# One decoder step on one core: the stick-breaking attention steps in another order, and one cast moved from DVE to ACT

## The chip, the cores and the metric

The kernel runs on one core of a Trainium2 chip. The metric is the device time of one execution, in microseconds. Before the change it is 2921.88 us, the median of three runs (2920.06 to 2928.34). All times below are in microseconds unless marked ns.

## The reference

The reference is one inference step of a small decoder with two layers. Layer 0 mixes tokens with a gated matrix product over chunks of 128 tokens, layer 1 with stick-breaking attention over keys and values shared by the layers of its kind; each is followed by a SwiGLU feed-forward layer. There are 1024 prompt tokens and 32 sample tokens (8 sequences of 4), a width of 1024, 16 heads of 64 and a hidden width of 2816. Everything is float32. The part that the change touches is the attention:

```python
z = jnp.einsum('bthd,bshd->bhts', q, k) * (HEAD_DIM ** -0.5) + bias     # scores
causal = k_pos[None, :] < q_pos[:, None]
log_beta = jax.nn.log_sigmoid(z)
log_rest = jnp.where(causal, jax.nn.log_sigmoid(-z), 0.0)
after = lax.cumsum(log_rest, axis=3, reverse=True) - log_rest
a = jnp.where(causal, jnp.exp(log_beta + after), 0.0)
out = jnp.einsum('bhts,bshd->bthd', a, v)
```

The weight of a key is exp(z - softplus(z) - the sum of softplus over all later keys). So each query needs a sum over the later keys, which the kernel forms with triangular matrices of -1 on TensorE, from the latest block of keys to the earliest.

## The kernel before

**Precision.** Each float32 matrix product is made of three products of fp32r parts: high by high, high by low, low by high. Who makes a high part rounds it with a copy or an activation, and who makes the low part subtracts the high part from the original. So each tile costs two elementwise passes, and each weight slab three on POOL (`w_hi`, the scaled `w_raw`, `w_lo`; lines 632 to 639).

**Stages.** The feed-forward layer of layer 0 ends at about 1150 us, the first key, query and value slab follows, attention runs from about 1187 to 2020, and the output projection and the second feed-forward layer fill the rest.

**The attention stage.** The 16 heads are worked on in 8 pairs. A pair has 12 steps s = 0 to 11 (`STEPS`, line 109). A step takes one block of 128 keys against up to 512 queries of the upper half (steps 0 to 7) or lower half (8 to 11) of the prompt, for two heads at once. Blocks on the diagonal are narrower: the widths are 128, 256, 384, 512, then 512 four times, then 128, 256, 384, 512. A tile of both heads has so 256 to 1024 elements in a partition. Each pair step is written out by hand for each engine, in a function `pair` of each, and the engines meet only at semaphores. For step s the chain is:

- PE `scores(s)` into PSUM (line 871)
- ACT `biased(s)`: scale and bias, into `zb` (1232)
- DVE `capped(s)`: minimum with 40, into `sp` (1553)
- ACT `exp_part(s)`, `log_part(s)`: the softplus, in place (1249, 1255)
- DVE `softplus(s)`: maximum with `zb` (1559)
- DVE `softplus_split(s)`: the cast to the high part (1570) and the low part by subtraction (1572), into `sp_part`
- PE `take_later(s)`: the triangular product of both parts, added to the running sums in PSUM (889)
- DVE `logits(s)`: that PSUM tile plus `zb` (1578)
- PE `carry(s)`: completes the block's contribution to the running sums (901), needs `logits(s)` to have read them
- ACT `weights(s)`: two exponentials, one to the high part in `a_part`, one in place (1242, 1243)
- POOL `a_low(s)`: the low part of the weights (644)
- PE `values(s)`: weights by values (916)

`sp_part` and `a_part` have one buffer each: the next high part of softplus may be written only when `carry` of the step before has read the last one, and the next `weights` only when `values` of the step before is done.

**Other work among the steps.** While one pair is in attention, PE projects the keys, queries and values of the next one, in nine chunks ("c" items, line 963, 24 matrix products of 384 or 288 columns each), turns key pages of the cache ("p"), and turns the projected keys and values to rows for output ("k", "v"). The tables `X1` and `X2` place these items in the steps: `X1` before `take_later`, `X2` behind it. DVE evicts each chunk (`chunk_evicted`, 1592) and makes low parts (`k_low`, 1604); ACT copies turned items and makes high parts (`k_high`, 1270). All items use one PSUM bank, `aux[:, 0]`, so an item can't begin before DVE or ACT has emptied the one before. POOL prepares the weight slabs in thirds (`split_part`) between its `a_low`. The 32 sample tokens have their own small chain (`sample`, `sample_values`, the `S_` constants). The last pair projects nothing; it restores earlier outputs instead (`o_back`, lines 1093 and 649).

The order within one step of a pair, before the change:

- PE: scores(s), values(s-3), carry(s-2), X1 item, take_later(s-1), X2 item, sample part
- ACT: biased(s), weights(s-2), exp_part(s), k_high, other copies, log_part(s), X2 item's copy
- DVE: logits(s-2), softplus(s-1), k_low, capped(s), cast and subtraction of s-1, chunk_evicted(s)
- POOL: a_low(s-2), a third of a slab in some steps

Lines of the PE, ACT and DVE programs with their numbers:

Of the kernel before, what the change touches and what calls it, by code (L numbers as in the profile page):

```python
# [23 lines left out]
ALU = mybir.AluOpType  # L24
# [58 lines left out]
def freed_by():  # L83
# [10 lines left out]
    for q0, t0 in zip(Q_FFN, T_FFN):  # L94
# [35 lines left out]
S_CAP, S_LOG, S_SOFT, S_LATER, S_EXP, S_VALUES = 8, 8, 9, 9, 10, 11  # L130
# [22 lines left out]
def yoco_step(nc, x_prompt, x_sample, cache_k, cache_v, page_table, norm_mix_g, a_w_in, a_v_g, a_ws, a_bs, a_w_out,  # L153
# [4 lines left out]
    with ExitStack() as ctx:  # L158
# [364 lines left out]
        def _(pool):  # L523
# [94 lines left out]
            gp.affine_select(out=s_mask[:], in_=s_mask[:], pattern=[[-DL, DB], [0, 2], [0, DL]], compare_op=ALU.is_ge,  # L618
                             fill=MASKED, base=0, channel_multiplier=1).then_inc(s_mask_done, 1)
# [32 lines left out]
            def pair(i, at, last_slabs=False, more=True):  # L652
                p, c = 2 * i + at, at % 2
                q = Q_KQV + 3 * (at + 1)
                for s in range(NS + (0 if more else 2)):
# [7 lines left out]
                    if more and s in (8, 9, 10):  # L663
                        split_part(s - 8, i, q + 3, None if last_slabs else G_KV, scaled + 3 * p + 2, 9 * p + 6)
# [21 lines left out]
        def _(pe):  # L686
# [311 lines left out]
            def sample_values(p, c):  # L998
                pe.wait_ge(s_ad, p + 1)
                pe.wait_ge(vp_in, 16 * DB * PAGES * (p + 1))  # L1000
                mm(os_, v_row[0:RS, RT, :], s_a[0:RS, 2, :], start=True, stop=False, skip_group_check=True)
                for n in range(DB * PAGES):
# [4 lines left out]
                last.then_inc(s_pv, 1)  # L1007

            def pair(p, c, more=True):
                for s in range(NS + (0 if more else 3)):  # L1010
                    if s < NS:
                        scores(p, c, s)
                    for lag, work in ((3, values), (2, carry)):
                        at = lagging(p, c, s, lag)
                        if at is not None:
                            work(*at)
                    if s in X1 and (more or X1[s][0] == "p"):
                        x_turn(p, c, X1[s], more)
                    if s == S_VALUES:
                        sample_values(p, c)  # L1020
# [5 lines left out]
                    sample(p, c, s)  # L1026

# [34 lines left out]
        def _(act):  # L1062
# [258 lines left out]
            def pair(p, c, more=True):  # L1321
                act.wait_ge(bias_done, p + 1)
                for s in range(NS + (0 if more else 3)):
# [21 lines left out]
                    if s == V_SPLIT:  # L1345
                        v_high(p)
# [56 lines left out]
        def _(dve):  # L1403
# [157 lines left out]
            def softplus_split(p, c, s):  # L1561
# [3 lines left out]
                if s > 0 and s - 1 in CARRY:  # L1565
                    dve.wait_ge(carry_done, NCARRY * p + CARRY.index(s - 1) + 1)
                elif s > 0 or not isinstance(p, int) or p > 0:
# [164 lines left out]
```

## Time and profile before

| What | Value |
|---|---|
| Median of three runs | 2921.88 us |
| The profiled execution's own time | 2921.54 us |
| Its span, first to last instruction | 2919.5 us |
| Mean granted TensorE clock | 0.955 of full speed |
| PE busy | 2763.1 us, 95% |
| DVE, ACT, POOL busy | 1350.9, 755.1, 1205.0 us |
| DMA engines, share of the span | 15.9% in the largest queue |

The span is one execution on the core; the device time has 2.0 us around it. PE busy is the time in which a matrix product was in the array, at whatever clock was granted. Idle time of an engine costs something only if the engine at the end of the chain waits for it. The granted clock has two levels, 2.4 GHz (1.00) and 1.2 GHz (0.50); a mean between them says for what share of a stretch it stood at the lower.

### The profile page before, as it was taken

The page shows a single profiled execution, that of the slowest core. Times are in us where ns is not written, and L with a number is a line of the kernel's source. Part 1 is how long each engine was busy: PE and PEld are TensorE (multiplying, and loading weights), DVE is VectorE, ACT ScalarE, POOL GpSimd, SP SyncE. Part 2 cuts the span into 40 slices and gives each one's busy share as a digit, 9 for nine tenths or more (in the row PEclk, how much of TensorE's full clock was granted, in tenths as well). Part 3 has the DMA queues.
Part 4 walks back from the last instruction along what each step waited for, and adds up shares of the span by engine and source line. Part 5 has one row for each costly group of instructions (what it writes and reads, how often), then busy time and mean ns, then how long its engine had stood idle before and what let it go on. Part 6 is the DMA issues. An engine that isn't in the chain of part 4 may idle for free.

```text
span 2919.5 us, 41661 instructions
## 1 busy us (share of the span) xinstructions
PE 2763.1 (95%) x16657; PEld 2637.8 (90%) x16657; DVE 1350.9 (46%) x1237; ACT 755.1 (26%) x1080; POOL 1205.0 (41%) x542
## 2 busy tenths in 40 slices
PE   7999999999999999899999999967999999999997
PEld 6989999999999999788787878756999999999997
DVE  5244543333333337566766766663543333333335
ACT  5122210000000002456665655653110000000003
POOL 4542454334433343344444444443454333433340
PEclk9999999999999999899988989966999999999999
DMA  3111111111111112221221122121121111111111
GB/s 111 51 31 37 44 58 45 51 44 44 44 51 44 44 44 94 61 61 39 64 60 36 53 66 63 32 91 67 43 59 44 46 50 44 44 44 51 44 37 60
DMA packets 219619, 152.91 MB, mean 52 GB/s; under 512 B 9258, under 2 KB 207714, under 8 KB 219426
## 3 DMA queue, kind: packets, MB, share of 16 engines
q1 hardware_dynamic: 200930, 139.63, 15.9%
q10 hardware_dynamic: 18496, 10.49, 1.2%
q8 instruction: 147, 2.41, 0.4%
q14 instruction: 46, 0.38, 0.0%
HBM read 128.86 MB, written 21.22 MB: 51 GB/s over the span
## 4 chain that ended last, share of the span: by engine, by line
PE 83%; DVE 6%; issue 5%; POOL 3%; ACT 2%; DMA 0%; ACTq 0%; SPq 0%; POOLq 0%; DVEq 0%
PE ps L706 48%; PE ps L835 17%; PE aux L963 6%; PE ps L889 2%; PE ps L916 2%; DVE sp_part L1572 2%; PE ps L871 2%; PE ps L901 2%; POOL a_part L644 1%; DVE scratch L1423 1%; PE aux L935 1%; PE aux L1005 1%; DVE sp_part L1570 1%; DVE sp L1559 1%; POOL w_raw L634 1%
## 5 line engine op out<-in xcount | busy, mean ns | idle before, releaser
L564 POOL TENSOR_TENSOR w_hi<-w_raw,ones_col 128x1024 fp32r<-128x1024 f32 x146 | 281.1, 1925 | 997.6 <-PE ps L706 674.2
L571 POOL TENSOR_TENSOR w_lo<-w_raw,w_hi 128x1024 fp32r<-128x1024 f32 x167 | 467.6, 2800 | 13.1
L644 POOL TENSOR_TENSOR a_part<-zb,a_part 128x256 fp32r<-128x256 f32 (+2 forms) x96 | 200.9, 2093 | 466.3 <-ACT zb L1243 466.3
L706 PE MATMUL ps<-near_hi,w_hi 128*128 128x352 f32 x1632 | 356.9, 327 | 17.0 <-DVE near_lo L1410 13.1
L706 PE MATMUL ps<-near_lo,w_hi 128*128 128x352 f32 x1632 | 354.2, 325 | 0.0
L706 PE MATMUL ps<-near_hi,w_lo 128*128 128x352 f32 x1632 | 352.8, 324 | 0.0
L706 PEld LDWEIGHTS ps<-near_hi,w_hi 128*128 128x128 f32 x1632 | 278.8, 190 | 21.1 <-issue 11.5
L706 PE MATMUL ps<-in_hi,w_hi 128*128 128x352 f32 x1320 | 286.6, 325 | 4.8 <-issue 3.9
L1537 DVE TENSOR_TENSOR h<-h,ps 128x1056 f32<-128x1056 f32 x160 | 200.2, 1251 | 187.3 <-PE ps L835 187.3
L706 PE MATMUL ps<-in_lo,w_hi 128*128 128x352 f32 x1320 | 285.3, 324 | 0.0
L706 PE MATMUL ps<-in_hi,w_lo 128*128 128x352 f32 x1320 | 283.9, 323 | 0.0
L706 PEld LDWEIGHTS ps<-near_hi,w_lo 128*128 128x128 f32 x1632 | 281.0, 189 | 0.0
L706 PEld LDWEIGHTS ps<-near_lo,w_hi 128*128 128x128 f32 x1632 | 279.2, 189 | 0.0
L1433 DVE TENSOR_TENSOR up<-ps,r_row 128x1056 f32<-128x1056 f32 x44 | 55.3, 1258 | 442.1 <-PE ps L706 442.1
L1193 ACT ACTIVATE gate<-gate 128x1056 f32<-128x1056 f32 x44 | 47.9, 1089 | 807.5 <-DVE gate L1433 807.5
L706 PEld LDWEIGHTS ps<-in_hi,w_hi 128*128 128x128 f32 x1320 | 224.7, 189 | 7.2 <-issue 5.3
L835 PE MATMUL ps<-hid_hi,w_hi 128*128 128x352 f32 x1056 | 228.4, 324 | 0.3 <-DVE h L1490 0.3
L835 PE MATMUL ps<-hid_lo,w_hi 128*128 128x352 f32 x1056 | 227.7, 324 | 0.0
L835 PE MATMUL ps<-hid_hi,w_lo 128*128 128x352 f32 x1056 | 227.2, 323 | 0.0
L706 PEld LDWEIGHTS ps<-in_hi,w_lo 128*128 128x128 f32 x1320 | 226.0, 188 | 0.0
L706 PEld LDWEIGHTS ps<-in_lo,w_hi 128*128 128x128 f32 x1320 | 224.8, 188 | 0.0
L1433 DVE TENSOR_TENSOR gate<-ps,r_row 128x1056 f32<-128x1056 f32 x44 | 55.3, 1258 | 320.0 <-PE ps L706 320.0
(218 smaller groups left out, 4501.2 us busy)
## 6 DMA issues: line engine op xcount, KB each, us to landing
w_raw<-in_w_gate_dram SPq DMA_DIRECT2D x44, 512.0 KB, 3.8
w_raw<-in_w_up_dram SPq DMA_DIRECT2D x44, 512.0 KB, 3.8
w_raw<-in_w_down_dram SPq DMA_DIRECT2D x44, 512.0 KB, 3.6
w_raw<-in_a_w_in_dram SPq DMA_DIRECT2D x16, 512.0 KB, 3.9
k_page<-in_cache_k_dram SPq DMA_DIRECT2D x128, 64.0 KB, 1.9
v_page<-in_cache_v_dram SPq DMA_DIRECT2D x128, 64.0 KB, 1.9
h_kept<-h SPq DMA_DIRECT2D x8, 528.0 KB, 2.7
h<-h_kept SPq DMA_DIRECT2D x8, 528.0 KB, 7.3
```

Of the source, the lines that this page charges most:

```text
L564: gp.tensor_tensor(hi, raw, one, ALU.mult).then_inc(w_hi_done, 1)
L571: gp.tensor_tensor(lo, raw, as32(hi), ALU.subtract).then_inc(w_ready, 1)
L644: gp.tensor_tensor(a_part[:, 1, :, c0:TB], zb[:, s % 3, :, c0:TB], as32(a_part[:, 0, :, c0:TB]), ALU.subtract).then_inc(a_split, 1)
L706: last = mm(out[:, c, 0:CH], w[:, ks], x[:, k, c * CH:c * CH + CH], start=(k == 0 and n == 0), stop=(k == KT - 1 and n == 2))
L835: last = mm(out[:, c, 0:CH], w[:, ns], x[:, buf, f, c * CH:c * CH + CH], start=(f == 0 and m == 0), stop=(f == 1 and m == 2))
L871: last = mm(ps[:, e, c0:TB], kq[rows, c, kn, P * j:P * j + P], kq[rows, c, qn, TB * b + c0:TB * b + TB], start=(m == 0), stop=(m == 2 and ...
L889: last = mm(ps[:, 2 + e, c0:TB], neg_tri_r[:], sp_part[:, x, e, c0:TB], start=(first and x == 0), stop=(x == 1), skip_group_check=True)
L901: last = mm(ps[:, 2 + e, c0:TB], neg_rest_r[:], sp_part[:, x, e, c0:TB], start=False, stop=(x == 1), skip_group_check=True)
L916: last = mm(ps[:, 4 + e, c0:TB], v_part[:, j, 2 * e:2 * e + 2, :].rearrange("p n d -> p (n d)"), a_part[:, x, e, c0:TB], start=(first and ...
L963: last = mm(xb[:, 0:CW[chunk]], w[:, ks], x[:, k, cols], start=(k == 0 and m == 0), stop=(k == KT - 1 and m == 2), skip_group_check=True)
L1433: vec.tensor_tensor(chunks(dst), ps[:, 3 * par:3 * par + 3, 0:CH], chunks(r_row[:]), ALU.mult)\
L1537: vec.tensor_tensor(chunks(h[:, n, :]), chunks(h[:, n, :]), ps[:, 3 * (n % 2):3 * (n % 2) + 3, 0:CH], ALU.add).then_inc(tile_out, 1)
```

## The change

The same reordered attention steps, and the cast of softplus to its high part on ACT instead of DVE. The order within one step of a pair after it:

- PE: scores(s), X1 item, half of the sample values in step 11, take_later(s-1), X2 item, sample part, the other half of the sample values in step 10, values(s-2), carry(s-1)
- ACT: weights(s-2), the cast `softplus_high(s-1)`, biased(s), exp_part(s), k_high, other copies, log_part(s), X2 item's copy
- DVE: softplus(s-1), the subtraction of s-1, v_low, capped(s), out, the sample's two, k_low, chunk_evicted(s), logits(s-1), sample_out
- POOL: as before, but the third slab's thirds stand in steps 7, 8, 9 and no longer in 8, 9, 10; and the three instructions that make the sample mask stand ahead of the five slabs of the first keys, queries and values

In the diff the first `pair` is PE's, `softplus_high` and the loop behind it are ACT's, and the last two parts are DVE's `softplus_split` and `pair`. The items of the tables `X1` and `X2` move too: chunks 5 to 7 and page item 3 come a step earlier, step 6 has now a chunk and a page item, step 9 has no chunk.

```diff
-X1 = {0: ("c", 0), 1: ("p", 1), 2: ("c", 1), 3: ("c", 2), 4: ("c", 3), 5: ("c", 4), 6: ("p", 3), 7: ("c", 5),
-      8: ("c", 6), 9: ("c", 7), 10: ("c", 8)}
-X2 = {0: ("p", 0), 2: ("k", 0), 3: ("k", 1), 4: ("k", 2), 5: ("p", 2), 9: ("v", 0), 10: ("v", 1), 11: ("v", 2)}
+X1 = {0: ("c", 0), 1: ("p", 1), 2: ("c", 1), 3: ("c", 2), 4: ("c", 3), 5: ("c", 4), 6: ("c", 5), 7: ("c", 6),
+      8: ("c", 7), 10: ("c", 8)}
+X2 = {0: ("p", 0), 2: ("k", 0), 3: ("k", 1), 4: ("k", 2), 5: ("p", 2), 6: ("p", 3), 8: ("v", 0), 9: ("v", 1),
+      11: ("v", 2)}
...
-S_CAP, S_LOG, S_SOFT, S_LATER, S_EXP, S_VALUES = 8, 8, 9, 9, 10, 11
+S_CAP, S_LOG, S_SOFT, S_LATER, S_EXP, S_VALUES = 8, 8, 9, 9, 10, (10, 11)
...
             ffn_splits(0)
-            for n in range(2):
-                scaled += 1
-                split(Q_KQV + n, 0, 0, n, (G_KV, G_MIX1)[n], scaled, 4 if n == 0 else 2)
-            for n in range(2, 5):
-                scaled += 1
-                split(Q_KQV + n, 0, 0, n % 2, (G_KV, G_MIX1, G_KV)[n % 3], scaled, 4 if n == 2 else 2)
-
-            pool.wait_ge(tile_done, T_KQV)
-            pool.wait_ge(sq_added, 4 * KT)
+            pool.wait_ge(sq_added, 3 * KT)
             gp.memset(s_mask[:], 0.0).then_inc(s_mask_done, 1)
...
+            for n in range(2):
+                scaled += 1
+                split(Q_KQV + n, 0, 0, n, (G_KV, G_MIX1)[n], scaled, 4 if n == 0 else 2)
...
...
-                    if more and s in (8, 9, 10):
-                        split_part(s - 8, i, q + 3, None if last_slabs else G_KV, scaled + 3 * p + 2, 9 * p + 6)
+                    if more and s in (7, 8, 9):
+                        split_part(s - 7, i, q + 3, None if last_slabs else G_KV, scaled + 3 * p + 2, 9 * p + 6)
...
             def pair(p, c, more=True):
-                for s in range(NS + (0 if more else 3)):
+                for s in range(NS + (0 if more else 2)):
                     if s < NS:
                         scores(p, c, s)
-                    for lag, work in ((3, values), (2, carry)):
-                        at = lagging(p, c, s, lag)
-                        if at is not None:
-                            work(*at)
                     if s in X1 and (more or X1[s][0] == "p"):
                         x_turn(p, c, X1[s], more)
-                    if s == S_VALUES:
-                        sample_values(p, c)
+                    if s == S_VALUES[1]:
+                        sample_values(p, c, 1)
...
                     sample(p, c, s)
+                    if s == S_VALUES[0]:
+                        sample_values(p, c, 0)
+                    for lag, work in ((2, values), (1, carry)):
+                        at = lagging(p, c, s, lag)
+                        if at is not None:
+                            work(*at)
...
+            def softplus_high(p, c, s):
+                b, j, c0 = STEPS[s]
+                if s > 0 and s - 1 in CARRY:
+                    act.wait_ge(carry_done, NCARRY * p + CARRY.index(s - 1) + 1)
+                elif s > 0 or not isinstance(p, int) or p > 0:
+                    act.wait_ge(c_done, NS * p + s)
+                act.wait_ge(sp_done, NS * p + s + 1)
+                nc.scalar.copy(sp_part[:, 0, :, c0:TB], sp[:, s % 2, :, c0:TB]).then_inc(sp_hi_done, 1)
...
-                    for lag, work in ((0, biased), (2, weights), (0, exp_part)):
+                    for lag, work in ((2, weights), (1, softplus_high), (0, biased), (0, exp_part)):
                         at = lagging(p, c, s, lag) if lag or s < NS else None
                         if at is not None:
                             work(*at)
+                        if s == V_SPLIT and work == weights:
+                            v_high(p)
...
-                vec.tensor_copy(hi, z).then_inc(sp_hi_done, 1)
                 dve.wait_ge(sp_hi_done, NS * p + s + 1)
                 vec.tensor_tensor(lo, z, as32(hi), ALU.subtract).then_inc(sp_split, 1)
...
-                for s in range(NS + (0 if more else 2)):
-                    for lag, work in ((2, logits), (1, softplus)):
-                        at = lagging(p, c, s, lag)
-                        if at is not None:
-                            work(*at)
+                for s in range(NS + (0 if more else 1)):
+                    at = lagging(p, c, s, 1)
+                    if at is not None:
+                        softplus(*at)
+                        softplus_split(*at)
+                    if s == V_SPLIT:
+                        v_low(p)
+                    if s < NS:
+                        capped(p, c, s)
+                    if s == OUT0 and (not isinstance(p, int) or p > 0):
+                        out(p - 1, 0)
+                    if s == OUT1:
+                        out(p, 1)
...
                         k_low(p, c, CHUNK_STEP[s - 2])
-                    if s < NS:
-                        capped(p, c, s)
-                    at = lagging(p, c, s, 1)
-                    if at is not None:
-                        softplus_split(*at)
                     if more and s in CHUNK_STEP:
                         chunk_evicted(p, c, CHUNK_STEP[s])
...
+                    if at is not None:
+                        logits(*at)
-                    if s == S_VALUES:
+                    if s == S_VALUES[1]:
                         sample_out(p)
```

## Rows read from the trace of the kernel before

**Rows 1.** Windows: pair 0, pair 6, the last pair; columns named in the first line.

```profile
core 0: us, PE busy (x) PEld busy (x) DVE busy (x) ACT busy (x) POOL busy (x), PEclk, DMA share, GB/s
1187.00:1290.00 103.00, 97.60 (x563) 86.05 (x564) 62.23 (x88) 58.97 (x98) 38.72 (x18) 0.87 0.15 42
...
1804.00:1905.00 101.00, 90.57 (x537) 77.76 (x535) 67.82 (x90) 61.55 (x101) 41.96 (x19) 0.92 0.19 55
1905.00:2020.00 115.00, 76.98 (x297) 59.03 (x297) 70.56 (x67) 61.45 (x86) 48.95 (x21) 0.62 0.28 92
```

**Rows 2.** PE's waits, 1187 to 2020: total us, times, longest.

```profile
PE ps L889 <- DVE sp_part L1572: 72.2, 33, 7.5
```

**Rows 3.** PE in order of time: start, us; idle before and releaser in brackets.

```profile
1186.52 0.91 PE L871 MATMUL ps<-kq 64*128 64x128 f32 x6 [4.53 <-POOL s_mask L618]
...
1541.66 2.07 PE L889 MATMUL ps<-sp_part,neg_tri_r 128*128 128x512 f32 x4 [4.29 <-DVE sp_part L1572]
```

**Rows 4.** Chain of waits through step 5 of pair 3: start, us, piece.

```profile
1525.70 0.89 PE ps L871 x6
1526.59 0.90 PE ps L916 x4
1527.49 0.92 PE ps L901 x4
1528.42 4.18 PE aux L963 x24
1532.60 0.94 PE ps L889 x4
```

**Rows 5.** ACT in order of time, the same step.

```profile
1527.48 1.26 ACT L1232 ACTIVATE zb<-ps,pair_bias 128x512 f32<-128x512 f32 x2 [1.22 <-PE ps L871]
1528.63 1.06 ACT L1242 ACTIVATE a_part<-zb 128x1024 fp32r<-128x1024 f32 x1
1529.58 1.05 ACT L1243 ACTIVATE zb<-zb 128x1024 f32<-128x1024 f32 x1
1530.53 1.05 ACT L1249 ACTIVATE sp<-sp 128x1024 f32<-128x1024 f32 x1
...
1531.88 1.06 ACT L1255 ACTIVATE sp<-sp 128x1024 f32<-128x1024 f32 x1
```

**Rows 6.** DVE in order of time, the same step, and the subtraction of the next.

```profile
1528.77 0.70 DVE L1553 TENSOR_SCALAR sp<-zb 128x1024 f32<-128x1024 f32 x1 [0.31 <-ACT zb L1232]
1529.38 0.69 DVE L1570 CAST sp_part<-sp 128x1024 fp32r<-128x1024 f32 x1
1530.10 1.23 DVE L1572 TENSOR_TENSOR sp_part<-sp,sp_part 128x1024 fp32r<-128x1024 f32 x1
...
1538.25 3.36 DVE L1572 TENSOR_TENSOR sp_part<-sp,sp_part 128x1024 fp32r<-128x1024 f32 x1
```

**Rows 7.** POOL in order of time beside these.

```profile
1530.71 2.89 POOL L644 TENSOR_TENSOR a_part<-zb,a_part 128x1024 fp32r<-128x1024 f32 x1 [3.76 <-ACT zb L1243]
1533.55 1.91 POOL L634 TENSOR_TENSOR w_raw<-w_raw,gains 128x1024 f32<-128x1024 f32 x1
1538.18 2.35 POOL L644 TENSOR_TENSOR a_part<-zb,a_part 128x1024 fp32r<-128x1024 f32 x1 [2.72 <-ACT zb L1243]
```

**Rows 8.** DVE in order of time, last pair: two neighbours on its queue.

```profile
1946.37 2.83 DVE L1570 CAST sp_part<-sp 128x1024 fp32r<-128x1024 f32 x1
1949.24 3.37 DVE L1572 TENSOR_TENSOR sp_part<-sp,sp_part 128x1024 fp32r<-128x1024 f32 x1
```

**Rows 9.** POOL in order of time beside them.

```profile
1945.96 2.70 POOL L644 TENSOR_TENSOR a_part<-zb,a_part 128x1024 fp32r<-128x1024 f32 x1 [1.20 <-ACT zb L1243]
1948.61 2.92 POOL L649 TENSOR_TENSOR in_lo<-o_back,in_hi 128x1056 fp32r<-128x1056 f32 x1
```

**Rows 10.** By source line, the DVE addition with a PSUM operand: ns min/median/max.

```profile
L1578 DVE TENSOR_TENSOR zb<-ps,zb x96: 414/1092/1226, 1200.2 to 2012.4; 128x1024 f32<-128x1024 f32 x48, 128x256 f32<-128x256 f32 x16, 128x512 f32<-128x512 f32 x16, 128x768 f32<-128x768 f32 x16
```

**Rows 11.** Groups by form, pairs 2 to 6: an ACT cast of 1024 elements.

```profile
L1310 ACT CAST v_part<-v_row 128x1024 fp32r<-128x1024 f32 x5 | 5.2, 1031 | 0.0
```

**Rows 12.** Windows of 4 us behind the stall of step 6.

```profile
1543.00:1547.00 4.00, 4.00 (x17) 3.04 (x17) 2.82 (x3) 0.13 (x1) 0.83 (x1) 0.50 0.49 118
1547.00:1551.00 4.00, 4.00 (x12) 3.23 (x13) 1.12 (x2) 3.21 (x5) 0.00 (x0) 0.53 0.31 87
```

More of the change, by code:

```diff
@@ L619, in _ @@
                              fill=MASKED, base=0, channel_multiplier=1).then_inc(s_mask_done, 1)
+            for n in range(2):
+                scaled += 1
+                split(Q_KQV + n, 0, 0, n, (G_KV, G_MIX1)[n], scaled, 4 if n == 0 else 2)
+            for n in range(2, 5):
+                scaled += 1
+                split(Q_KQV + n, 0, 0, n % 2, (G_KV, G_MIX1, G_KV)[n % 3], scaled, 4 if n == 2 else 2)
             def split_part(part, i, at, gain, n_scaled, used):
@@ L996, in sample, with sample_values @@
                        skip_group_check=True).then_inc(s_c, 1)
[L998 to L1002, printed above, removed]
+            def sample_values(p, c, half):
+                if half == 0:
+                    pe.wait_ge(s_ad, p + 1)
+                    pe.wait_ge(vp_in, 16 * DB * PAGES * (p + 1))
+                    mm(os_, v_row[0:RS, RT, :], s_a[0:RS, 2, :], start=True, stop=False, skip_group_check=True)
+                for n in range(half * DB, half * DB + DB):
                     b, j = divmod(n, PAGES)
@@ L1006, in sample_values @@
                               start=False, stop=(n == DB * PAGES - 1), skip_group_check=True)
-                last.then_inc(s_pv, 1)
+                if half == 1:
+                    last.then_inc(s_pv, 1)
             def pair(p, c, more=True):
-                for s in range(NS + (0 if more else 3)):
+                for s in range(NS + (0 if more else 2)):
                     if s < NS:
                         scores(p, c, s)
-                    for lag, work in ((3, values), (2, carry)):
-                        at = lagging(p, c, s, lag)
-                        if at is not None:
-                            work(*at)
                     if s in X1 and (more or X1[s][0] == "p"):
                         x_turn(p, c, X1[s], more)
-                    if s == S_VALUES:
-                        sample_values(p, c)
+                    if s == S_VALUES[1]:
+                        sample_values(p, c, 1)
                     at = lagging(p, c, s, 1)
@@ L1322, in pair @@
                 act.wait_ge(bias_done, p + 1)
-                for s in range(NS + (0 if more else 3)):
-                    for lag, work in ((0, biased), (2, weights), (0, exp_part)):
+                for s in range(NS + (0 if more else 2)):
+                    for lag, work in ((2, weights), (1, softplus_high), (0, biased), (0, exp_part)):
                         at = lagging(p, c, s, lag) if lag or s < NS else None
@@ L1564, in softplus_split @@
                 hi, lo = (sp_part[:, x, :, c0:TB] for x in range(2))
-                if s > 0 and s - 1 in CARRY:
-                    dve.wait_ge(carry_done, NCARRY * p + CARRY.index(s - 1) + 1)
-                elif s > 0 or not isinstance(p, int) or p > 0:
-                    dve.wait_ge(c_done, NS * p + s)
-                dve.wait_ge(sp_done, NS * p + s + 1)
-                vec.tensor_copy(hi, z).then_inc(sp_hi_done, 1)
                 dve.wait_ge(sp_hi_done, NS * p + s + 1)
@@ L1653, in pair @@
                         k_low(p, c, CHUNK_STEP[s - 2])
-                    if s < NS:
-                        capped(p, c, s)
-                    at = lagging(p, c, s, 1)
-                    if at is not None:
-                        softplus_split(*at)
                     if more and s in CHUNK_STEP:
                         chunk_evicted(p, c, CHUNK_STEP[s])
-                    if s == V_SPLIT:
-                        v_low(p)
-                    if s == OUT0 and (not isinstance(p, int) or p > 0):
-                        out(p - 1, 0)
-                    if s == OUT1:
-                        out(p, 1)
-                    if s == S_VALUES:
+                    if at is not None:
+                        logits(*at)
+                    if s == S_VALUES[1]:
                         sample_out(p)
```

2 lines of the change are left out of this document (removed).

## The prediction

> **What bounds the kernel now.** I read the windows first, one for each pair of attention. From 1187 to 1905 there are seven pairs that also project, 718 us or 102.6 us each; the reader is to see that PE is busy nearly all of such a window and yet runs at a mean clock of 0.87 to 0.92 [rows 1]. Outside attention the edit touches only the sample mask. Then PE's waits: in the stage PE waits above all for the subtraction that makes the low part of softplus, 72 us in 33 waits [rows 2]. Then the order of time: the largest of these in a pair is in step 6, which has no chunk, 4.29 us [rows 3], and behind it PE works for a while at the lower of its two clock levels, 0.50 against 1.00 [rows 12]. So a pair has three parts. In pair 0, PE idles 103 - 97.6 = 5.4 us; a mean clock of 0.87 says that 26% of the time was at the lower level, which costs half of that, 13.4 us; 84 us are work at full clock. In pair 6 the same sum is 101 - 10.4 - 8.1 = 82.5 us. That floor, some 84 us, is what the new order could reach if nothing made PE wait: 7 x 18.6 = 130 us less.
>
> **The mask, at the start.** PE waits 4.53 us for POOL's three small instructions before the first scores [rows 3]. Ahead of the slabs they are done early: POOL has nothing there that PE needs sooner, and `sq_added` at 24 was reached before the feed-forward layer. The chunk of step 0 needs the fourth slab, which is ready by then. That gives back 4.5 us, and part of the lower clock behind the wait, for which I take 2.5 us: -7 us, once (bounds: 0, if step 0 then waits for something else, and -9).
>
> **The moved cast.** On DVE it takes 0.69 us for 1024 elements [rows 6]; on ACT such a cast takes 1.03 us [rows 11]. ACT is busy 60 of 103 us in a pair [rows 1], so in busy time it has room, eight wide and four narrower casts adding some 11 us. But ACT works in order, and the cast stands between `weights` and `biased`. What counts is the ring of waits that the new order closes.
>
> **The ring, for a full-width step with a slab third on POOL.** Let 0 be the start of `weights(s-2)` on ACT. Two exponentials of 0.95 us each from start to start end at 2.0, `softplus_high` at 2.95 [rows 5, 11]. POOL's `a_low(s-2)` begins at 2.05. Here the rows show something that the old order mostly avoided. A DVE instruction whose operands are all in SBUF does not run beside a POOL instruction: the subtraction that takes 1.23 us alone takes 3.36 us when `a_low` began 0.07 us before it, and when DVE came first, `a_low` takes 2.89 instead of 2.35 us [rows 6, 7]. In the old order the subtraction began 0.6 us ahead of `a_low`; in the new one it can't begin before the ACT cast ends at 2.95, 0.9 us behind `a_low`. So it waits to 4.4 and ends at 5.6. In nine of the twelve steps (0, 1, 4 to 9, 11) POOL then has a slab third ready. The rows of the last pair show who goes first: the cast waits for `a_low`, then POOL's next instruction runs, and only then the DVE subtraction, so the two alternate [rows 8, 9]. The third takes 1.9 us [rows 7], to 7.5 (2.35 us for the subtracting third). Only then comes `capped(s)`, now behind the subtraction on DVE: to 8.1. Then `exp_part` to 9.15, 0.4 us for `k_high`, `log_part` to 10.6 and half a microsecond for the copy of the turned item, since ACT goes on in order: the next `weights` begins at 11.1 at the earliest. DVE instructions with a PSUM operand are never longer than their own time, 1.23 us at most in 96 [rows 10], so `logits` and the evictions are not held.
>
> PE needs 0.89 + 4.18 + 0.94 + 0.90 + 0.92 = 7.8 us for such a step [rows 4], with the turned item and the sample part 8.2 to 9.1. Its wait is at two places: for the subtraction, and at the X2 item, since the eviction of the chunk is behind `capped` on DVE and all items share one bank. In the old order `capped(s)` ran beside `weights` and the ring did not close.
>
> The Trainium skill has the holding as a rule: in "SBUF — State Buffer", section "SBUF: two separate sides", the pair of ports that DVE and GpSimd share is an exclusive lock, kept for the whole instruction by whoever starts first, for DVE instructions with two SBUF inputs or in a two-port mode. The trace agrees (3.36 against 1.23 us, rows 6). It doesn't say who goes next when both wait; by that rule alone the third would not come between, and a step would take about 9.4 us, which is a rival below.
>
> **Twelve steps.** I carried the ring through a pair at full clock with these durations, narrower tiles in proportion (the addition spans 0.41 to 1.23 us from 256 to 1024 elements [rows 10]). Steps 4, 5, 6: 10.7, 12.2, 12.2 us. Step 7, without a turned item: 10.3. Step 8, with a narrow tile: 9.6. Step 9 has no chunk: `take_later(8)` waits for the `weights(7)`, `a_low(7)` and the subtraction, and the sample part for a DVE instruction behind `capped`, 10.6. Steps 10 and 11: 8.3 and 7.0. Step 0: 11.2. Step 1: 8.4, since `values(11)` now comes two steps behind its scores and waits for 2.0 + 2.35 us of weights with 2.5 us of work before it. Step 2: 11.8, since `out` of the pair before stands ahead of the eviction and waits for two ACT copies. Step 3: 7.0. Sum 119.3 us, of which 84 to 86 is work. The idle stretches of 2.5 to 4 us next to short instructions will bring the lower clock, as the stall of step 6 did [rows 12]; most of its cost falls into PE's waits. I add 3 us: 122 us for a pair, 118.5 for pair 0, in which POOL has no thirds in steps 0 and 1. Against 718 us that is 6 x 122 + 118.5 = 850.5, +132 us.
>
> **The last pair** took 115 us [rows 1] and has `o_back` instructions on ACT and POOL in place of chunks. The ring is the same with a longer POOL instruction, 2.4 us without its wait [rows 9], about 12.3 us in steps 5 to 8; against that, splitting the sample values and one lag step less at the end save some 4 us. I take +3 (bounds -10 and +15).
>
> Sum: -7 + 132 + 3 = +128 us. The profiled execution took 2921.5 us, 0.3 from the median of 2921.9, so about 3049 us, +4.4%.
>
> **Rivals.**
> - Only `a_low` holds DVE, and the thirds fit into later gaps (the rule's case). Full steps then take 9.2 to 10.4 us, the pair 103.5, with the clock 105: +17 us for seven pairs, -7 at the start, near 2933, between 2912 and 2960. For it: four evictions and `logits` in a step are free of POOL. Against it: rows 8 and 9. Chance 0.17.
> - The other side: the holds cost PE nothing, because chunks of 4.18 us cover them. This decides if the subtraction ends less than 6 us behind the start of `weights` and `capped` follows at once: the ACT ring is then 2.0 + 1.0 + 1.25 + 0.65 + 1.05 + 0.4 + 1.0 + 0.6 = 8.0 us, below PE's 8.5, and what stays are the short steps 1, 2 and 9, some 7 us, and 3 us of clock: 96 us for a pair, -46 -7 = -53, near 2868; without these stalls near 2785. For it: step 6 gets a chunk, the 4.29 us go, and the sample values no longer stand in one piece. The Trainium skill speaks for it too: "Perfetto Trace Analysis", section "Optimizing Scalar/DVE Operations", says that moving work from a saturated DVE to Scalar may make sense. But DVE is busy 62 to 68 of 101 to 103 us in these pairs [rows 1], not saturated. Against it: the subtraction must start behind `a_low` in each step. Chance 0.14.
> - The clock stays at the lower level for most of a pair. Work of 84 us with half of its chunks at that level gives about 135 us for a pair: near 3140. For it: the last pair, with a stall in each step, has 0.62 [rows 1]. Chance 0.09.
> - My forecast: 0.60, with its own range 2985 to 3095.
>
> **How the numbers follow.** The likeliest case gives 3049. A measurement tells this kernel from no change at about 0.3%, or 9 us. The faster chance is the second rival and hardly any of the first, 0.15; within 0.3% lies a part of the first, 0.06; the rest is slower, 0.79. The range from 2920 to 3100 holds the forecast, nearly all of the first rival and little of the third, about 0.8.
>
> **What would show it.** In the changed kernel's trace, windows of a pair of about 122 us with PE busy under 90% and a clock under 0.87; L1572's subtraction at a mean above 2.3 us for 1024 elements, and `capped` at about 2.5 us in full steps, where it was 0.69; PE waiting for the subtraction and for `staged` (the eviction) in each of steps 4 to 9; no wait for the mask. Were `capped` still near 0.7 us, the alternation would be wrong; were the subtraction at 1.23 us, the order of ACT and POOL within the ring; were PE's waits small with both long, the cover. The time of a pair decides between the cases: 96, 105, 122 or 135 us.

## The result and the profile after

The changed kernel takes 3096.82 us, the median of four runs (3094.29 to 3099.47), against 2921.18 us before. The ratio is 1.0596, with a 95% interval of 1.0577 to 1.0615: 176 us slower, where 128 us were forecast. The span grew from 2919.5 to 3092.4 us, by 172.9 us.

The windows of the changed kernel: one of a middle pair, one of the last pair, with the columns of [rows 1].

```profile
1551.00:1678.00 127.00, 105.99 (x552) 89.15 (x553) 78.32 (x75) 68.60 (x108) 47.04 (x21) 0.82 0.13 37
...
2065.00:2193.00 128.00, 87.00 (x334) 65.74 (x333) 70.00 (x60) 76.45 (x108) 46.08 (x22) 0.62 0.28 91
```

A middle pair has grown to 127 us or more, PE is busy 83% of it, and the mean clock fell to 0.82. From the start of each pair's first scores in the order of time: the seven pairs took 705.8 us before (97.5 for pair 0, 101.4 each for pairs 1 to 6) and take 883.4 us now (111.8, and 128.6 each). The first scores start at 1181.94 instead of 1186.52 [rows 3]. From the last pair's first scores to the output projection it is 127.8 us before and 127.7 now. -4.6 + 177.6 - 0.1 = 172.9 us: the whole loss lies in the seven pairs that also project.

PE's waits from 1187 to 2200, total us, times, longest; the row before is [rows 2]:

```profile
PE ps L889 <- DVE sp_part L1579: 84.1, 35, 4.1
PE aux L969 <- DVE staged L1599: 35.5, 19, 2.4
PE aux L924 <- DVE staged L1599: 32.1, 20, 2.1
```

The wait for the subtraction has grown from 72.2 us. The two waits for an eviction, at the X2 items, were 3.9 us together before and are 68 us now. The waits are only part of the loss. Pairs 1 to 6 as one window, before and after:

```profile
1284.02:1892.35 608.33, 564.30 (x3327) 491.61 (x3326) 415.05 (x541) 363.67 (x588) 276.42 (x125) 0.91 0.18 53
```

```profile
1293.76:2065.32 771.56, 647.15 (x3325) 542.05 (x3325) 476.61 (x469) 419.48 (x662) 279.43 (x125) 0.81 0.14 42
```

With the prediction's three parts this is, for a pair before, 7 us in which PE idles, 9 us that the lower clock level costs, and 85 us of work at full clock. After the change it is 21, 24 and 83 us. So of 27 us more in a pair, half or a little more shows as lower clock and the rest as idle time.

The groups by form say which instructions grew. First the stretch from 1400 to 1900 of the kernel before, then 1400 to 2080 of the changed one; behind the busy time stands the mean ns of one.

```profile
L1572 DVE TENSOR_TENSOR sp_part<-sp,sp_part 128x1024 fp32r<-128x1024 f32 x30 | 56.4, 1879 | 1.0
...
L1553 DVE TENSOR_SCALAR sp<-zb 128x1024 f32<-128x1024 f32 x30 | 20.8, 692 | 12.9 <-ACT zb L1232 12.9
```

```profile
L1579 DVE TENSOR_TENSOR sp_part<-sp,sp_part 128x1024 fp32r<-128x1024 f32 x31 | 74.2, 2392 | 91.8 <-ACT sp_part L1256 91.8
...
L1566 DVE TENSOR_SCALAR sp<-zb 128x1024 f32<-128x1024 f32 x31 | 66.1, 2132 | 5.3 <-ACT zb L1236 5.2
```

The subtraction went from 1.88 to 2.39 us on average, and `capped`, the same instruction on the same data, from 0.69 to 2.13 us. Neither does more work. Step 5 of pair 3 in the order of time shows the ring; first ACT:

```profile
1602.94 1.06 ACT L1246 ACTIVATE a_part<-zb 128x1024 fp32r<-128x1024 f32 x1 [1.15 <-issue]
1603.91 1.04 ACT L1247 ACTIVATE zb<-zb 128x1024 f32<-128x1024 f32 x1
1604.86 1.04 ACT L1256 CAST sp_part<-sp 128x1024 fp32r<-128x1024 f32 x1
1605.80 1.25 ACT L1236 ACTIVATE zb<-ps,pair_bias 128x512 f32<-128x512 f32 x2
1610.86 1.06 ACT L1262 ACTIVATE sp<-sp 128x1024 f32<-128x1024 f32 x1 [3.81 <-DVE sp L1566]
...
1612.23 1.05 ACT L1268 ACTIVATE sp<-sp 128x1024 f32<-128x1024 f32 x1
1613.19 0.56 ACT L1295 COPY k_page_t<-aux 128x512 f32<-128x512 f32 x1
1614.76 1.06 ACT L1246 ACTIVATE a_part<-zb 128x1024 fp32r<-128x1024 f32 x1 [1.01 <-PE ps L916]
```

Then POOL, DVE and PE beside it:

```profile
1605.03 2.41 POOL L644 TENSOR_TENSOR a_part<-zb,a_part 128x1024 fp32r<-128x1024 f32 x1 [6.54 <-ACT zb L1247]
1607.39 2.89 POOL L634 TENSOR_TENSOR w_raw<-w_raw,gains 128x1024 f32<-128x1024 f32 x1
```

```profile
1605.93 2.60 DVE L1579 TENSOR_TENSOR sp_part<-sp,sp_part 128x1024 fp32r<-128x1024 f32 x1 [3.28 <-ACT sp_part L1256]
1608.45 2.38 DVE L1566 TENSOR_SCALAR sp<-zb 128x1024 f32<-128x1024 f32 x1
...
1611.17 0.55 DVE L1599 TENSOR_TENSOR staged<-aux,r_row 128x384 f32<-128x384 f32 x1
```

```profile
1608.58 1.20 PE L889 MATMUL ps<-sp_part,neg_tri_r 128*128 128x512 f32 x4 [0.94 <-DVE sp_part L1579]
1611.85 1.11 PE L969 MATMUL aux<-ident,k_page 128*128 128x128 f32 x4 [2.07 <-DVE staged L1599]
1612.61 2.05 PE L916 MATMUL ps<-a_part,v_part 128*128 128x512 f32 x4
```

The reader is to see the alternation. The subtraction, ready at 1605.93, waits until `a_low` ends at 1607.44; the slab third on POOL, queued at 1607.39, waits until the subtraction ends at 1608.5; `capped`, queued at 1608.45, waits until the third ends at 1610.3. Only then can ACT go on (its idle 3.81 us). PE waits twice, and the products behind the second wait take 2.05 us, where the same four take 1.2 us at full clock (1.20 us at 1506.05).

### The profile page after: what moved, and what is told of

The parts are those of the page before. It is cut to its first block, busy times and chain, and to the rows that moved or that the text cites. A ratio compares the mean times of both kernels' runs of the same rounds, so it can differ in the third digit from the quotient of the medians.

```text
span 3092.4 us, 41657 instructions
## 1 busy us (share of the span) xinstructions
PE 2851.2 (92%) x16657; PEld 2687.0 (87%) x16657; DVE 1415.2 (46%) x1141; ACT 829.0 (27%) x1176; POOL 1206.5 (39%) x542
## 4 chain that ended last, share of the span: by engine, by line
PE 69%; issue 15%; DVE 7%; ACT 4%; POOL 4%; ACTq 0%; DMA 0%; DVEq 0%; POOLq 0%; SPq 0%
PE ps L706 44%; PE ps L835 16%; DVE sp L1566 2%; PE ps L916 2%; PE aux L963 1%; POOL a_part L644 1%; ACT sp_part L1256 1%; DVE scratch L1436 1%; POOL w_raw L634 1%; POOL w_lo L639 1%; POOL w_hi L632 1%; ACT zb L1247 1%; PE ps L871 1%; PE ps L889 1%; DVE sp_part L1579 1%
## 5 line engine op out<-in xcount | busy, mean ns | idle before, releaser
L572 POOL TENSOR_TENSOR w_lo<-w_raw,w_hi 128x1024 fp32r<-128x1024 f32 x167 | 468.8, 2807 | 13.1
L644 POOL TENSOR_TENSOR a_part<-zb,a_part 128x256 fp32r<-128x256 f32 (+2 forms) x96 | 176.2, 1835 | 618.0 <-ACT zb L1247 618.0
L1579 DVE TENSOR_TENSOR sp_part<-sp,sp_part 128x256 fp32r<-128x256 f32 (+2 forms) x96 | 184.2, 1919 | 258.7 <-ACT sp_part L1256 258.7
```

The lines of the kernel that those rows point to most:

```text
L572: gp.tensor_tensor(lo, raw, as32(hi), ALU.subtract).then_inc(w_ready, 1)
L644: gp.tensor_tensor(a_part[:, 1, :, c0:TB], zb[:, s % 3, :, c0:TB], as32(a_part[:, 0, :, c0:TB]), ALU.subtract).then_inc(a_split, 1)
L1579: vec.tensor_tensor(lo, z, as32(hi), ALU.subtract).then_inc(sp_split, 1)
```

## The experiments

**1. The change taken apart.** The first four kernels run parts of the change.

The first is the changed kernel with the cast back on DVE:

```diff
-                    for lag, work in ((2, weights), (1, softplus_high), (0, biased), (0, exp_part)):
+                    for lag, work in ((2, weights), (0, biased), (0, exp_part)):
...
+                dve.wait_ge(sp_done, NS * p + s + 1)
+                vec.tensor_copy(hi, z).then_inc(sp_hi_done, 1)
                 dve.wait_ge(sp_hi_done, NS * p + s + 1)
```

> The changed kernel with one part undone: the cast of softplus to its high part is again on DVE, directly ahead of the subtraction; the new order of the steps, the tables, the mask and the halves of the sample values stay. Theory (the ring of waits through ACT, the port that DVE and POOL share, and PE): the cast no longer waits for the two exponentials, so the subtraction begins about where a_low begins, and the ACT ring of a full step shortens from 11.1 to about 9 us; but capped and k_low still stand behind a_low and a slab third, so a pair falls from 128.6 to about 116 us, and the kernel takes 2990 to 3030 us, still slower than before. Rival (the moved cast is the cause, the order is good): a pair of 96 to 101 us, 2870 to 2920 us.

Measured: 3005.18 us, ratio to before 1.0282 (1.0267 to 1.0298), pairs 1 to 6 at 116.2 us each. The theory held, the rival fell: the new order loses without the moved cast. Here the subtraction has a mean of 1.56 us and `capped` of 1.77 us.

The second is the kernel before with the cast alone moved:

```diff
-                    for lag, work in ((0, biased), (2, weights), (0, exp_part)):
+                    for lag, work in ((0, biased), (1, softplus_high), (2, weights), (0, exp_part)):
...
-                vec.tensor_copy(hi, z).then_inc(sp_hi_done, 1)
```

> The kernel before with the cast alone moved to ACT, between biased and weights; old order of the steps. Theory (order is what closes the ring): in the old order a_low begins behind the subtraction even with the cast on ACT, since weights comes behind the cast; capped runs beside. ACT gets 0.95 us more in a full step and stays below PE's 8.3 us: 2920 to 2950 us, the pair 101 to 105 us. Rival (the cast on ACT is the cause, 1 us in each of 96 steps and more by waits): 3000 us or more.

Measured: 2889.81 us, ratio 0.9883 (0.9864 to 0.9902). The rival fell, and the theory had the wrong sign: in the old order the moved cast is a gain of 32 us. The groups by form of this kernel, the same stretch as before:

```profile
L1575 DVE TENSOR_TENSOR sp_part<-sp,sp_part 128x1024 fp32r<-128x1024 f32 x30 | 36.8, 1225 | 21.4 <-ACT sp_part L1252 20.6
```

The subtraction takes 1.23 us on average instead of 1.88. The cast on ACT stands ahead of the exponentials, so `a_low` starts later, and no subtraction of full width meets it any more. In the stretch shown part of the hold moves to `softplus`, the maximum (1.34 to 1.72 us), but in step 6 of pair 3 the subtraction ends 5.5 us after the scores begin, where it was 7.7, and step 6 falls from 11.2 to 8.1 us. The same edit holds the port for the one in the new order and frees it for the other in the old.

The third kernel has all the small parts of the change, and neither the order nor the cast:

```diff
+X1 = {0: ("c", 0), 1: ("p", 1), 2: ("c", 1), 3: ("c", 2), 4: ("c", 3), 5: ("c", 4), 6: ("c", 5), 7: ("c", 6),
+      8: ("c", 7), 10: ("c", 8)}
...
                     sample(p, c, s)
+                    if s == S_VALUES[0]:
+                        sample_values(p, c, 0)
```

> The kernel before with all the small parts of the change and neither the new order within a step nor the moved cast: the tables X1 and X2 with a chunk in step 6 and none in step 9, the third slab in steps 7 to 9, the mask ahead of the slabs, the sample values in halves in steps 10 and 11. Theory: the 4.3 us wait of step 6 and the lower clock behind it go, step 9 gets a wait of 1 to 2 us, the one long piece of narrow products goes: a pair of 92 to 96 us, 2850 to 2890 us. Rival (the wait only moves from step 6 to step 9): 2905 to 2920 us.

Measured: 2894.41 us, ratio 0.9906 (0.9892 to 0.9920), pairs at 98.8 us. Between the two: about half of the forecast gain. Step 9 fell from 8.1 to 4.9 us without its chunk, but step 6 still took 10.2 us with one, and step 10 with half of the sample values 9.3 instead of 6.6 us.

The fourth kernel has the mask alone ahead of the slabs (the hunk in `ffn_splits` of the diff).

> The kernel before with the sample mask alone made ahead of the slabs. Theory: the wait of 4.53 us ahead of the first scores goes and part of the lower clock behind it, 5 to 9 us less, 2912 to 2916 us. Rival: the first step waits for something else instead, no change within 0.1%.

Measured: 2915.52 us, ratio 0.9980 (0.9970 to 0.9989), 6.5 us less. The theory held, and with it the term of -7 us.

So from before to after: the small parts -28 us (2922 to 2894), the order +111 (to 3005), the cast on top of it +92 (to 3097).

**2. The hold of the port, taken away.** Two kernels have the changed order and cast, and less work on POOL. They leave out work that the result needs, so they serve only to show what holds what. The first cuts all three thirds of a slab as this line shows for one:

```diff
-                    gp.tensor_tensor(hi, raw, factor, ALU.mult).then_inc(w_hi_done, 1)
+                    gp.tensor_tensor(hi[:, 0:1, :], raw[:, 0:1, :], factor[:, 0:1, :], ALU.mult).then_inc(w_hi_done, 1)
```

> The changed kernel, with POOL's slab thirds in attention cut to one of their eight column blocks (the other seven are not prepared, so this leaves out most of the preparation of the slabs for pairs 2 to 7 and the first of the output projection). Theory (a_low and a slab third in turn hold capped and k_low): without the thirds' hold the ring of a full step falls from 11.1 to about 9.3 us, capped falls below 1 us, a pair to 104 to 112 us, the kernel to 2930 to 3000 us. Rival (what costs is the cast and the exponentials in order on ACT, and the thirds fit in gaps): 3060 us or more.

Measured: 3005.21 us, ratio 1.0289 (1.0273 to 1.0304), pairs 1 to 6 at 115.3 us, just outside what was expected (2930 to 3000 us, pairs of 104 to 112) and far below the rival. The groups by form, from 1400 to 1900:

```profile
L1579 DVE TENSOR_TENSOR sp_part<-sp,sp_part 128x1024 fp32r<-128x1024 f32 x25 | 59.8, 2394 | 66.3 <-ACT sp_part L1256 66.3
...
L1566 DVE TENSOR_SCALAR sp<-zb 128x1024 f32<-128x1024 f32 x25 | 20.8, 834 | 4.9 <-ACT zb L1236 4.9
```

The subtraction is as long as before (2.39 us), since `a_low` still holds it; `capped` is back at 0.83 us. So the two holds are separate, and that of the thirds was worth 92 us of the 176. The full steps 4 to 8 take 8.7, 10.1, 10.0, 9.3 and 7.8 us; the short steps 1 and 9 still 10.1 and 11.2.

Then the low part of the weights is cut as well, with its rest set to zero once:

```diff
-                gp.tensor_tensor(a_part[:, 1, :, c0:TB], zb[:, s % 3, :, c0:TB], as32(a_part[:, 0, :, c0:TB]),
+                gp.tensor_tensor(a_part[:, 1, :, c0:c0 + 64], zb[:, s % 3, :, c0:c0 + 64],
```

> The changed kernel with the thirds cut as before and with the low part of the weights made for 64 of up to 512 columns only (the rest of that part is zero, so most of the low by high product of weights and values is left out). Theory: with no hold of the port the ring is 8.0 us and PE with 8.2 to 9 us sets the full steps; the short steps 1, 2 and 9 keep waits: a pair of 95 to 102 us, 2865 to 2925 us, so the whole loss is the port. Rival (the new order loses by its own waits even with a free port): 2960 us or more.

Measured: 2931.97 us, ratio 1.0044 (1.0028 to 1.0061), pairs 106.6 us. The time is 7 us above what was expected and well below the rival. Its groups by form, from 1400 to 1900:

```profile
L1582 DVE TENSOR_TENSOR sp_part<-sp,sp_part 128x1024 fp32r<-128x1024 f32 x29 | 35.5, 1226 | 76.8 <-ACT sp_part L1259 76.8
...
L1569 DVE TENSOR_SCALAR sp<-zb 128x1024 f32<-128x1024 f32 x29 | 20.1, 695 | 8.9 <-ACT zb L1239 8.9
```

Both DVE instructions take their own time, and the full steps 4 to 8 take 8.7, 8.7, 8.4, 9.3 and 7.1 us, which is PE's work. Of the 176 us, 165 went with POOL's instructions. `a_low`, though, is also in the chain to `values`, so a shorter one shortens a plain wait too; this kernel doesn't separate that part. The whole loss is not the port, as the theory had it. The kernel has the small parts and the moved cast, which are gains in the old order: the same parts in the old order, with all of POOL's work, take 2886 us (experiment 5). So some 46 us or more are the order's own, with the port nearly free. They stand above all in steps 1, 3, 9 and 11, with 6.6, 8.6, 8.8 and 10.0 us, where that kernel has 4.1, 6.8, 5.1 and 7.5. No kernel has the thin instructions in the old order, so what the hold cost there isn't known.

**3. The lower clock.** The changed kernel with more work on PE:

```diff
+            def fill(p, s, n):
+                pe.wait_ge(zb_done, NS * p + s + 1)
+                for _ in range(n):
+                    mm(ps[:, 0, 256:512], neg_tri_r[:], in_hi[:, 0, 0:256], start=True, stop=True,
+                       skip_group_check=True)
...
+                    if more and s in (1, 9):
+                        fill(p, s, 12)
...
+                    if more and s in (0, 2, 5, 6, 8):
+                        fill(p, s, 12)
```

> The changed kernel with 12 products of 256 columns more on PE, at places where it waits: ahead of take_later in steps 1 and 9, ahead of the X2 item in steps 0, 2, 5, 6 and 8. Their result is overwritten unread. Theory (the term for the clock was too small, 3 us for a pair where 8 to 10 were lost, since the lower level delays values and with it the next exponentials on ACT): the clock in a pair rises from 0.81 to 0.88 or more and a pair loses 3 to 6 us: 3055 to 3080 us. Rival (the lower clock lies within the waits and costs nothing, the 6 us a pair are ring waits that the sum left out): 3090 us or more, by 1.3 us of work seven times a pair where the wait is shorter than that.

Measured: 3064.22 us, ratio to before 1.0487 (1.0472 to 1.0501), 33 us less than the changed kernel, with 84 products more in each pair. One window of its pair 3 and one of pair 5:

```profile
1550.00:1673.00 123.00, 107.19 (x647) 91.95 (x646) 81.00 (x81) 70.34 (x112) 47.20 (x21) 0.93 0.14 43
1800.00:1925.00 125.00, 110.47 (x661) 94.49 (x660) 79.55 (x80) 70.95 (x112) 47.25 (x21) 0.92 0.14 43
```

The mean clock in a pair rises from 0.81 to 0.92 and pairs 1 to 6 fall from 128.6 to 122.6 us. In the three parts a pair has now 15 us idle, 10 us for the lower level, and 97 us of work, of which the added products are 12.5. So the lower level costs 14 us less and PE idles 5 us less, against the added work, and 6 us came back. At least 6 us in a pair were not hidden in the waits.

**4. Who starts first.** The changed kernel with one line other, the cast ahead of the exponentials:

```diff
-                    for lag, work in ((2, weights), (1, softplus_high), (0, biased), (0, exp_part)):
+                    for lag, work in ((1, softplus_high), (2, weights), (0, biased), (0, exp_part)):
```

> The changed kernel with one line changed: on ACT the cast stands ahead of the two exponentials of weights instead of behind them. Theory (who starts first gets the port): the subtraction now begins before a_low and takes its own 1.23 us again, but capped, which waits for biased behind the weights, still meets a_low; the ring of a full step is about 10.2 us: a pair of 120 to 124 us, 3035 to 3070 us, with the subtraction at a mean below 1.5 us. Rival (the place of the cast on ACT doesn't matter, only its 1 us): within 0.3% of 3097 us.

Measured: 3078.83 us, ratio to before 1.0533 (1.0509 to 1.0557), between theory and rival. DVE in the order of time, from 1611 on, in a middle pair:

```profile
1611.50 1.22 DVE L1579 TENSOR_TENSOR sp_part<-sp,sp_part 128x1024 fp32r<-128x1024 f32 x1 [1.50 <-ACT sp_part L1256]
1614.56 1.85 DVE L1566 TENSOR_SCALAR sp<-zb 128x1024 f32<-128x1024 f32 x1 [1.83 <-ACT zb L1236]
1616.33 2.71 DVE L1611 TENSOR_TENSOR kq<-staged,kq 128x384 fp32r<-128x384 f32 x1
```

The subtraction has its own 1.22 us again (mean 1.226 over 24): that part of the theory held. What was missed: `capped` at 1.85 us still waits for `a_low`, and then `k_low` (2.71 us, 0.55 alone) waits for the slab third, with the eviction behind it. The hold moved to the next DVE instruction. The cast, too, waits for `carry` now.

**5. Towards a better kernel.** All of the change but the order:

```diff
-                    for lag, work in ((2, weights), (1, softplus_high), (0, biased), (0, exp_part)):
+                    for lag, work in ((0, biased), (1, softplus_high), (2, weights), (0, exp_part)):
...
```

On PE and DVE the old order is back as well.

> The kernel before with the small parts (tables, mask, halves of the sample values) and the cast on ACT between biased and weights, in the old order of the steps: all of the change but the order. Theory: the two gains, 27 us of the small parts and 32 us of the cast alone, lie at different steps and add up to most of their sum: 2855 to 2875 us. Rival (both take the same wait of step 6 away): 2880 to 2895 us.

Measured: 2886.15 us, ratio 0.9875 (0.9854 to 0.9896). The rival held: the small parts and the cast don't add up. Step 6 is 8.3 us in this kernel and 7.5 to 8.7 with the cast alone; the cast has taken its stall away without a chunk.

Then, without the tables and the halves, the kernel before with cast and mask only:

> The kernel before with the cast on ACT between biased and weights, and the mask ahead of the slabs; tables and sample values as before. Theory (the two edits lie apart and add): 2880 to 2886 us, 4 to 9 us below the cast alone.

Measured: 2881.44 us (2871.77 to 2889.94), ratio 0.9865 (0.9841 to 0.9890). Within what was expected, and the lowest median of all: 41 us below before, 215 us below the change. Its interval overlaps those of the cast alone and of the kernel with all but the order, so that the two edits add isn't firm. With the tables as well:

> The same with the tables X1 and X2 and the third slab's steps of the change as well, and the sample values in one piece in step 11. Theory (the halves put a narrow piece with a wait into step 10, 11.8 us in place of 6.6 for a shorter step 11, and that took the tables' gain away): 2865 to 2880 us. Rival (the tables give nothing once the cast is moved): 2880 to 2890 us.

Measured: 2891.87 us, ratio 0.9894 (0.9875 to 0.9913). Above both ranges: with the cast on ACT the tables give no gain, and the halves of the sample values were not what took it away. The intervals of these two kernels overlap, so a loss of about 10 us isn't firm. And with eight products more in steps 1 and 11 of the kernel with cast and mask:

> The kernel with cast and mask, and 8 products of 256 columns more on PE ahead of take_later in step 1 and in the middle of the sample values in step 11, result overwritten unread. Theory (narrow products and short waits there let the clock fall for steps 0 and 2): each costs up to 0.9 us and gives 1.5 to 3 us back, 5 to 15 us below the kernel with cast and mask. Rival (the clock falls all the same): 5 to 12 us above it.

Measured: 2891.96 us, ratio 0.9893 (0.9873 to 0.9912). The gain of the theory is not there, and the median lies in the rival's range, but this loss isn't firm either, since the intervals overlap. The clock doesn't explain it: over all executions the mean granted clock is 0.959 to 0.964 with the filling and 0.956 to 0.967 without. In step 1 PE idles 0.7 us without the filling, in step 11 0.2 us, while the places filled in experiment 3 had 0.8 to 4.8 us. That this is why the filling gains nothing here wasn't tested.

## Why the prediction was right, and where it fell short

**What bounds it.** The windows said that PE is the bound and its waits for the subtraction the lever; after the change the same wait leads, with the evictions behind it, but no wait is as large as what the lower clock costs.

**The mask.** Forecast -7, measured -6.5 us alone. Right.

**The ring.** Right to some tenths. From the start of the exponentials at 1602.94: `a_low` ends at 4.5 (forecast 4.4), the subtraction at 5.6 (5.6), the third at 7.3 (7.5), `capped` at 7.9 (8.1), `exp_part` at 9.0 (9.15), `log_part` at 10.3 (10.6), the copy at 10.8 (11.1). The signs named beforehand were there: the subtraction at 2.39 us (above 2.3), `capped` at 2.13 (about 2.5; four of the six full steps in a pair have 2.38 us or more, and step 3, which has no third, 0.69), PE waiting for the evictions, no wait for the mask, a clock of 0.82 (under 0.87). That POOL's third comes between two DVE instructions was taken from two rows [rows 8, 9]; the kernel with thin thirds, at 3005 us, shows it at work. The rule's case, the first rival, forecast 2933 and so fell, and the second with it. The third, a lower clock for most of a pair, didn't fall as clearly: it had pairs of 135 us, the forecast 122, and 128.6 lies between them, with the clock at the lower level in 38% of a pair. The kernel's 3097 us are 2 us outside the forecast's own range, whose end is 3095, and 3 us inside the wide one. That the wide range still holds it is luck. The Trainium skill's exclusive lock ("SBUF — State Buffer", section "SBUF: two separate sides") agrees with all of these runs (with both POOL instructions thin the subtraction is back at 1.23 us); the turn-taking behind it isn't on that page. The thirds, which get their turn by it, were worth 92 us here.

**The twelve steps.** Forecast at full clock, the mean over pairs 1 to 6 from the starts of the scores, and the mean granted clock in each step:

| Step | 0 | 1 | 2 | 3 | 4 | 5 | 6 | 7 | 8 | 9 | 10 | 11 | Sum |
|---|---|---|---|---|---|---|---|---|---|---|---|---|---|
| Forecast | 11.2 | 8.4 | 11.8 | 7.0 | 10.7 | 12.2 | 12.2 | 10.3 | 9.6 | 10.6 | 8.3 | 7.0 | 119.3 |
| Measured | 10.8 | 9.9 | 12.4 | 8.8 | 9.8 | 13.5 | 13.1 | 9.9 | 9.1 | 12.5 | 9.2 | 9.5 | 128.6 |
| Clock | 0.81 | 0.66 | 0.78 | 0.78 | 1.00 | 0.86 | 0.85 | 0.96 | 0.97 | 0.61 | 0.84 | 0.63 | 0.81 |

The three steps with a clock of 0.96 or more came out 0.4 to 0.9 us below the forecast. All others but step 0 came out above it, by 0.6 to 2.5 us.

**The term that was mis-sized** is "I add 3 us" for the lower clock, with the reason that "most of its cost falls into PE's waits". The lower level costs 24 us in a pair. If all of the 9.3 us between 119.3 and 128.6 are its doing, 15 of the 24 lie in waits; what was left over is then three times the term, and the filled kernel shows at least twice. One way from the clock to the ring is that PE works at the lower level behind a wait, and what it does there is `values`, which the next exponentials on ACT wait for. The row of 1614.76 shows it: ACT had ended its copy at 1613.75 and waited 1.01 us for `values`, which took 2.05 us in place of 1.2. The window around it:

```profile
1611.00:1615.00 4.00, 3.15 (x11) 2.68 (x12) 3.07 (x4) 2.99 (x5) 0.00 (x0) 0.57 0.00 0
```

Of the 9.3 us in a pair the filled kernel gave 6 back; for the rest, 3.3 us, a share of the clock that filling didn't reach and waits left out of the sum are both possible, and no run tells them apart. So pairs 1 to 6 came out at 128.6 where 122 were forecast: 40 us more; pair 0 at 111.8 where 118.5 were: 7 us less.

**A second term** was the base: the windows from 1187 to 1905 took 12.7 us of the last pair into the seven, so 718 us stood where 705.8 was right. That made the forecast difference 12 us too small. The last pair was forecast at +3 and gave 0, and not by the forecast's ring. Steps 5 to 8 take 10.0, 11.4, 10.9 and 7.6 us there, where about 12.3 were forecast. The `o_back` instruction on POOL waits for ACT, starts behind `capped`, and so doesn't come between it and the subtraction:

```profile
2122.95 2.18 DVE L1579 TENSOR_TENSOR sp_part<-sp,sp_part 128x1024 fp32r<-128x1024 f32 x1 [1.17 <-ACT sp_part L1256]
2125.05 0.68 DVE L1566 TENSOR_SCALAR sp<-zb 128x1024 f32<-128x1024 f32 x1
```

```profile
2127.86 2.46 POOL L649 TENSOR_TENSOR in_lo<-o_back,in_hi 128x1056 fp32r<-128x1056 f32 x1 [3.81 <-ACT in_hi L1097]
```

So that +3 was near is luck. Together 33 + 12 + 2 - 3 us, with the start at -4.6 instead of -7, is the 45 us between 128 and 173.

**What wasn't foreseen** is that the two named parts pull in opposite ways. The prediction priced the cast only within the new order. It gains 32 us in the old one, although DVE is busy only 69 of 101 us. The Trainium skill, in "Perfetto Trace Analysis", section "Optimizing Scalar/DVE Operations", says that such a move may make sense when DVE is saturated. Here the cast itself got longer, 1.05 us on ACT for 0.69 on DVE, and most of the gain stands in step 6, where the subtraction no longer meets a hold of 2.1 us.

## What to carry to other kernels

Where two engines exclude each other, the cost of an instruction is its place: look in the order of time at which of the two starts first, and take a duration far above the shortest of its form as a sign of a hold. When a change makes an instruction wait for another engine, write the whole ring out, with what POOL has queued behind it, before counting busy time. And price a lower clock by what waits for PE's next results, not by PE's own slack. Run the parts of a change one at a time: here one part was good and hidden by another.

## What the runs showed of the hardware

DVE and POOL took turns instruction by instruction when both had work queued: in the ring, subtraction 1.5 us behind `a_low`, third 1.1 us behind the subtraction, `capped` 1.8 us behind the third. In attention, in the traces of the kernels before and after, of the cast alone and of the cast ahead of the exponentials, no POOL instruction above 0.6 us has more than one DVE instruction with all operands in SBUF end within it. The single-input instruction `capped` was held like the two-input subtraction (2.38 us against 0.69), while instructions with a PSUM operand kept their time beside POOL. In the kernel before, nearly all evictions of a chunk of 384 columns ran wholly beside a POOL instruction (the one at 1532.64 beside `a_low`, 1530.71 to 1533.60), and their mean from 1400 to 1900 is their own time:

```profile
L1592 DVE TENSOR_TENSOR staged<-aux,r_row 128x384 f32<-128x384 f32 x29 | 16.2, 558 | 50.1 <-PE aux L963 50.1
```

More work made the kernel faster: 84 products of 256 columns in each pair, in seven steps in which PE idled 0.8 to 4.8 us, raised the mean clock from 0.81 to 0.92 and took 33 us off. In the faster kernel, where PE idled 0.7 and 0.2 us in the two steps filled, eight products in each had no gain.
